# A hybrid encoder layer: a new order of the feed-forward's first tiles on PE, DVE, ACT and POOL

## The reference, cut to what matters

```python
def _dwconv3(h, conv_w, conv_b):
    hp = jnp.pad(h, ((0, 0), (1, 1), (0, 0)))
    return hp[:, :-2] * conv_w[0] + h * conv_w[1] + hp[:, 2:] * conv_w[2] + conv_b

    x = x + jnp.concatenate([attn, pool], axis=-1) @ w_out
    up = _dwconv3(_rmsnorm(x, norm2) @ w_up, conv_w, conv_b)
    gate, val = up[..., :D_FF], up[..., D_FF:]
    x = x + (jax.nn.silu(gate) * val) @ w_down
```

## Time and profile before

| | |
|---|---|
| median of 3 runs | 1142.33 us |
| profiled execution: time, span | 1145.8 us, 1144.0 us |
| PE busy | 1117.0 us (98%) |
| DVE busy | 833.3 us (73%) |
| ACT, POOL busy | 555.3 us (49%), 466.8 us (41%) |
| mean granted clock of PE | 0.994 of full |
| feed-forward's first tiles | about 371 to 442 us of the span |

### The profile page before, as it was taken

The page is one execution under the profiler, slowest core; times in us unless marked ns, Lnnn a source line. Parts: engine busy times, 40 slices in busy tenths (PEclk is TensorE's granted clock), DMA queues, the critical chain, the costliest instruction groups (busy, mean ns, idle before and its releaser), DMA issues.

```text
span 1144.0 us, 15838 instructions
## 1 busy us (share of the span) xinstructions
PE 1117.0 (98%) x5146; PEld 898.0 (78%) x5146; DVE 833.3 (73%) x1171; ACT 555.3 (49%) x986; POOL 466.8 (41%) x405
## 2 busy tenths in 40 slices
PE   8999999999999989999999999999999999999996
PEld 7788766665878867888888888888888888888885
DVE  6895976674468799878787878787876756757555
ACT  5412687775223454545454445444554545544332
POOL 0186642322567046765686568655220202211000
PEclk9999999999999999999999999999999999999999
DMA  6601000104653126443544354444896565534341
GB/s 208 222 26 44 1 12 12 38 19 168 200 185 120 56 64 220 165 139 136 194 165 138 138 193 165 138 141 173 326 349 205 186 200 189 180 100 127 92 143 74
DMA packets 138431, 161.60 MB, mean 141 GB/s; under 512 B 8755, under 2 KB 105354, under 8 KB 133770
## 3 DMA queue, kind: packets, MB, share of 16 engines
q1 hardware_dynamic: 138080, 160.82, 42.1%
q10 hardware_dynamic: 298, 0.11, 0.0%
HBM read 115.55 MB, written 45.35 MB: 141 GB/s over the span
## 4 chain that ended last, share of the span: by engine, by line
PE 84%; DVE 11%; issue 2%; ACT 1%; POOL 1%; DMA 1%; ACTq 0%; DVEq 0%; POOLq 0%
PE ps L312 26%; PE ps L313 25%; PE ps L314 25%; PE ps L885 2%; PE ps L866 2%; DVE WL L2076 1%; DVE SF L2175 1%; DVE SF L2183 1%; PE ps L877 1%; DVE XL L1745 1%; DVE WDHL L1933 1%; DMA TL<-g_scratch 1%; DVE col L1944 1%; DVE XT L1739 0%; DVE R L1926 0%
## 5 line engine op out<-in xcount | busy, mean ns | idle before, releaser
L312 PE MATMUL ps<-XH,WH 128*128 128x512 f32 x722 | 284.0, 393 | 1.4 <-DVE WL L353 1.0
L314 PE MATMUL ps<-XH,WL 128*128 128x512 f32 x722 | 281.4, 390 | 0.0
L313 PE MATMUL ps<-XL,WH 128*128 128x512 f32 x722 | 281.3, 390 | 0.0
L312 PEld LDWEIGHTS ps<-XH,WH 128*128 128x128 f32 x722 | 135.9, 188 | 31.1 <-DVE WL L353 1.8
L314 PEld LDWEIGHTS ps<-XH,WL 128*128 128x128 f32 x722 | 135.6, 188 | 28.5
L313 PEld LDWEIGHTS ps<-XL,WH 128*128 128x128 f32 x722 | 135.9, 188 | 27.2
L312 PE MATMUL ps<-GHL,WH 128*128 128x512 f32 x394 | 153.7, 390 | 1.0 <-DVE WL L2076 0.7
L314 PE MATMUL ps<-GHL,WL 128*128 128x512 f32 x394 | 153.3, 389 | 0.0
L313 PE MATMUL ps<-GHL,WH 128*128 128x512 f32 x394 | 153.3, 389 | 0.0
L348 ACT ACTIVATE WH<-WR 128x1024 fp32r<-128x1024 f32 (+3 forms) x45 | 45.5, 1012 | 135.8 <-PE ps L314 122.7
L1492 ACT ACTIVATE SF<-ps,col 128x512 f32<-128x512 f32 x88 | 68.2, 778 | 74.7 <-PE ps L314 65.6
(11 more groups left out here) (259 smaller groups left out, 2263.7 us busy)
## 6 DMA issues: line engine op xcount, KB each, us to landing
TL<-in_w_up SPq DMA_DIRECT2D x48, 256.0 KB, 3.5
s_scratch<-XT SPq DMA_DIRECT2D x11, 1024.0 KB, 4.7
XT<-in_w_down SPq DMA_DIRECT2D x11, 1024.0 KB, 6.5
t_scratch<-XT SPq DMA_DIRECT2D x11, 1024.0 KB, 3.8
WR<-t_scratch SPq DMA_DIRECT2D x44, 256.0 KB, 2.8
TL<-s_scratch SPq DMA_DIRECT2D x44, 256.0 KB, 2.9
WR<-in_w_up SPq DMA_DIRECT2D x40, 256.0 KB, 3.4
WR<-in_w_down SPq DMA_DIRECT2D x33, 256.0 KB, 3.5
```

The costliest lines, as they stand in the source:

```text
L312: pe.matmul(out, wh, xh, start=first, stop=False, skip_group_check=skip)
L313: pe.matmul(out, wh, xl, start=False, stop=False, skip_group_check=skip)
L314: return pe.matmul(out, wl, xh, start=False, stop=last, skip_group_check=skip)
```

## The change

Six edits, all around the first tiles:

- PE: the four pairs of sums by ones stood one behind the other; now an inner step of `whole(0)` (three matmuls) stands between each two pairs, three steps in all.
- ACT: one element goes through Silu ahead of the second sequence's high halves, so that the table is loaded there. Three high halves of "7" come before `copy_m5`, behind a wait for the end of `whole(3)`. The high halves of two weights come between those of "4". The weights of "6" and "5" come ahead of the activations, and `silu(0, 1, 1)` goes into the next block.
- DVE: the low half 14 comes ahead of the first taps; 15 and 16 come between the low halves of "4"; 17 and 18 between and behind the taps of tiles 2 and 3; the last two pairs of taps of f = 1 go into the next block, around its low half 20, and `add_c22` goes ahead of 21 and 22 there.
- POOL: the wait for all low halves of "4" (`b_lo` 32) ahead of the weight sums of step 1 goes.

```diff
@@ PE, sums by ones
                 ins = pe.matmul(ps[6][:, TT + t:TT + t + 1], SQT[:, t * P:(t + 1) * P], ones[:, 0:1], start=False, stop=True)
+                if t < TT - 1:
+                    whole(0, [2 + t])
             ins.then_inc(ss_ready, 1)
-            whole(0, range(2, KT))
+            whole(0, range(5, KT))
@@ ACT
             up_hi(quarter(1, 1), raw_in[1][1], 32, wo_ready, 2 * KT, 3)
+            act.activation(col[:, FR:FR + 1], ones[:, 0:1], ACT.Silu)
...
             whole_centre(0)
+            act.wait_ge(m_done, WHOLE_DONE[3])
+            for k in range(3):
+                piece_hi(MOVE["7"][0][:, k, :], xt[:, XS[1], k, :], tp_ready, k + 1)
             copy_m5(0, 1, False)
             up_hi(s1_buf(0), ws_ready, 8, m_done, entry_at("5"), 1)
-            for k in range(4):
-                piece_hi(MOVE["7"][0][:, k, :], xt[:, XS[1], k, :], tp_ready, k + 1)
+            piece_hi(MOVE["7"][0][:, 3, :], xt[:, XS[1], 3, :], tp_ready, 4)
...
                 piece_hi(MOVE["4"][0][:, k, :], xt[:, XS[0], 4 + k, :], t4_ready, k + 1)
-            up_hi(quarter(0, 1), raw_in[0][1], 64, m_done, entry_at("2"), 3)
-            up_hi(quarter(0, 0), raw_in[0][0], 64, m_done, entry_at("7"), 0)
-            for c in range(2, 4):
-                whole_centre(c)
+                if k == 0:
+                    up_hi(quarter(0, 1), raw_in[0][1], 64, m_done, entry_at("2"), 3)
+                if k == 1:
+                    up_hi(quarter(0, 0), raw_in[0][0], 64, m_done, entry_at("7"), 0)
+            whole_centre(2)
             up_hi(S2, ws_ready, 10, m_done, entry_at("3"), 1)
+            whole_centre(3)
+            up_hi(s1_buf(0), ws_ready, 9, m_done, entry_at("4"), 2)
             silu(0, 0, 0)
             silu(0, 0, 1)
             gate0(0, 1, False)
-            up_hi(s1_buf(0), ws_ready, 9, m_done, entry_at("4"), 2)
...
             copy_m1(1, 0)
-            silu(0, 1, 1)
...
                 gate0(i, f, copied=copied)
+                if copied:
+                    silu(0, 1, 1)
@@ DVE
             piece_lo("7", 3, xt[:, XS[1], 3, :])
+            up_lo(quarter(1, 3), 2, 14)
...
                 piece_lo("4", k, xt[:, XS[0], 4 + k, :])
-            up_lo(quarter(1, 3), 2, 14)
-            for k in range(2, 4):
-                piece_lo("4", k, xt[:, XS[0], 4 + k, :])
             up_lo(quarter(0, 1), 3, 15)
+            piece_lo("4", 2, xt[:, XS[0], 6, :])
             up_lo(quarter(0, 0), 0, 16)
-            for c in range(2, 4):
-                tap_left(0, 0, c)
-                tap_right(0, 0, c)
+            piece_lo("4", 3, xt[:, XS[0], 7, :])
+            tap_left(0, 0, 2)
+            tap_right(0, 0, 2)
             up_lo(S2, 1, 17)
+            tap_left(0, 0, 3)
+            tap_right(0, 0, 3)
+            up_lo(s1_buf(0), 2, 18)
             product(0, 0, 1)
             product(0, 0, 0)
-            tap_left(0, 1, 0)
-            tap_right(0, 1, 0)
-            up_lo(s1_buf(0), 2, 18)
-            for c in range(1, 4):
+            for c in range(2):
                 tap_left(0, 1, c)
                 tap_right(0, 1, c)
...
                 if behind:
+                    tap_left(0, 1, 2)
+                    tap_right(0, 1, 2)
                     up_lo(quarter(f, 1), UP_SLOT["3"], i * 14 + (base + 6))
+                    tap_left(0, 1, 3)
+                    tap_right(0, 1, 3)
+                    add_c22(i, f)
...
-                add_c22(i, f)
+                if not behind:
+                    add_c22(i, f)
@@ POOL
             pool.wait_ge(uw_lo, 13)
-            pool.wait_ge(b_lo, 32)
```

## The result

The changed kernel takes 1149.68 us (median of 6 runs, 1146.79 to 1151.15) where the kernel before takes 1142.28 (6 runs beside it): the ratio is 1.005, 95% interval 1.0036 to 1.0065, that is 5.7 us slower (4.1 to 7.4). The two medians alone lie 7.4 us apart, at the upper end of that interval; in the larger sets beside the experiments the kernel before has medians of 1143.7 to 1144.0. The profiled execution has a span of 1147.4 us against 1144.0.

A forecast was written before the change was run, and what follows sets the result against it. PE, busy 98% of the span, bounds the kernel, with DVE setting the pace in the feed-forward's first tiles. Terms 0.0 + 3.2 + 0.8 = +4.0 us on the median 1142.33 gave 1146.3, range 1138.0 to 1149.0.

The forecast's parts named there:

- Part 1: Sums by ones on PE: spacing holds the clock, but the gain goes into waiting for the diagonal; 0.0 us.
- Part 2: High halves in ACT's gaps: DVE 0.6 us earlier, POOL's four sums start at 408.6 instead of 409.22.
- Part 3 at "4": DVE's low halves take turns with POOL's sums, 1.68 us each; product "4" comes 2.0 us later.
- Part 3 at "1" of the second block: DVE's low half for product "1" lands at 444.6 against 441.17, and PE waits; term +3.2 us.
- 1.0 us in which DVE waits for ACT: Added to DVE's time before the second block: ACT work queued behind the weight that waits for "4".
- The clock: Behind "4", PE falls to 1.2 GHz after two waits of 2.5 us; +0.8 us, bounds 0 and +2.
- DVE keeps the port: Rival at "4": DVE's six instructions end near 416 and the order works as drawn; -5.8, 1136.5; chance 0.16.
- Fewer collisions: Rival: "4" ends near 421 but DVE makes it up before the second block; +1.5, 1143.8; chance 0.18.
- The clock falls at the spread too: Rival to the spaced sums: clock falls at the spread, 1.7 us later for all behind; +5.7, 1148.0; chance 0.06.

The follow-up runs named there:

- kernel 1: Changed kernel with POOL's wait for all low halves of "4" put back ahead of its weight sums; ratio to the kernel before 1.0036.
- kernel 3: Changed kernel with POOL's four weight sums taken over 4 columns instead of 512, the rest left uncomputed; ratio to the kernel before 1.0003.
- kernel 4: Changed kernel with the last two pairs of taps and the sum of blocks put back ahead of the block; ratio to the kernel before 1.0022.
- 6: Changed kernel with both POOL's wait and the last two pairs of taps put back; ratio to the kernel before 1.0007.
- kernel 2: Kernel before with only POOL's wait for the low halves of "4" removed; ratio to the kernel before 1.0008.
- 10: Kernel before with only the last two pairs of taps, their block sum and activation moved into the block; ratio to the kernel before 1.0018.
- 11: Kernel before with only the sums by ones spaced by three groups of three matmuls; ratio to the kernel before 1.0008.
- 12: 9 with the change's three groups of matmuls in the sums by ones instead of one; ratio to the kernel before 0.998.
- 7: Kernel before with only one group of three matmuls in the middle of the sums by ones; ratio to the kernel before 1.0006.
- 9: Second reordering of DVE and ACT, POOL waiting for three halves of "4", one matmul group in the sums; 1139.48 us against 1143.96 before, ratio 0.9962.
- 8: First reordering of DVE and ACT, POOL waiting for three halves of "4", one matmul group in the sums; ratio to the kernel before 0.9993.

## Why the prediction was right in its direction and low in its size

Forecast: 4.0 us slower, 1146.3, range 1138.0 to 1149.0. Measured: 5.7 slower by the ratio, which on the forecast's base of 1142.33 is 1148.0, inside the range; the median of 1149.68 itself lies 0.7 us above it.

- **Part 1, 0.0: right, the reason half right.** F went from 7.62 to 7.32, with no slow matmul and a wait of 1.18 us where 1.3 was forecast; the 0.3 us are that the sums ended 2.06 us later and not 2.34. What I had wrong is the clock's fall as a fixed property of sums in a row: it came in two of four profiles.
- **Part 2, DVE 0.6 us earlier: right.** POOL's four sums start at 405.95 + 2.35 = 408.30 (forecast 408.6), the first half of "4" at 412.23 (412.5). Of the 0.92 us by which the four sums are earlier, 0.30 is the shorter F, which leaves 0.6.
- **Part 3 at "4": right nearly to the tenth.** On the clock of before, POOL's first weight sum starts at 414.16 (forecast 414.3), DVE's instructions stand 1.68 apart (1.68), the last half ends at 421.46 (421.6), and PE takes it at 421.51 (421.65). The Trainium skill's "SBUF — State Buffer", section "Who interferes with whom", has the loser wait for the whole instruction; by that I had estimated a turn of 1.97 us. The row's 1.68 decides: that one engine blocks the other is as the Trainium skill says, the price of a turn is not. Kernels 1 and 3 show that POOL's sums are the cause.
- **Part 3 at "1" of the second block: mechanism right, too small.** The weight landed at 443.75 + 2.35 = 446.10, forecast 444.6. The term that failed is "1.0 us in which DVE waits for ACT": DVE stood still for 0.93 + 1.96 + 0.64 = 3.53, the first two for ACT and the last for PE. The clock and the taps make this together: without the slow matmuls behind "4" it is 0.93 (kernel 3), with the taps back in their place 0.41 (kernel 4). The slow matmuls made product "5" late, which the sum needs; and I had counted the taps as moved work, not as work that before filled DVE's waits. The collisions behind came out 1.0 us under mine (0.94, 1.09, 0.7 and 0.2 for three of 1.08 and 0.7), which is no more than the kernel before had there (2.93 us in both). That the wait of 2.19 us came out inside the forecast's 2 to 3 is partly luck: PE, too, was late there, at 441.70 + 2.35 = 444.05 where 441.4 was forecast, about what thirteen slow matmuls cost (2.6 us). From the spread to this product PE lost 66.45 - 61.66 = 4.8 us, against 3.2 + 0.8: roughly 4.0 us are waits for DVE (7.64 against 3.63), about 1.0 is thirteen slow matmuls behind "4" instead of eight.
- **The clock, +0.8 with a bound of +2: right behind "4", missed at the second place.** It fell twice. The spell behind "4" (419.2 to 424.4, clock 0.50) I had foreseen, and it costs 1.0 us more than that of before; the one behind the wait of 2.19 us at "1" of the second block I had not, though I forecast that very wait at 2 to 3 us and had a row with a fall behind 2.15 us. Its eight slow matmuls cost 1.6 us, but the kernel before waits 0.55 us there for a block's sum, and the changed one does not: a hundred matmuls further on the changed kernel has lost 0.8 of the 5.75 - 4.8 + 0.3 = 1.25 us that are left. The other 0.4 lies later and is not explained. Kernel 4, where that wait is gone, has no slow matmuls there, and neither has 6.
- **Rivals.** "DVE keeps the port" fell: none of the five instructions ran at 0.68. "Fewer collisions" fell: DVE made nothing up, its weight landed 4.9 us later than before. "The clock falls at the spread too" did not come: behind that wait the clock held in seven profiles of seven.

How far the causes add up: alone in the kernel before, the wait costs 0.9 us, the taps 2.1 and the spaced ones 0.9 (the first and last not told from nothing), 3.9 in all, against 5.7. With intervals of 1 us and more to either side on each of these, the two are not clearly apart. That the causes make each other worse is argued from the traces and not shown by the times: in the new order two weights stand among the halves of "4" under POOL's sums, and there POOL's wait is worth 4.3 us of PE's waits in "4" (5.4 against 1.1, kernel 1), in the old order 1.1 (kernel 2). I have not split the rest further.

## What to carry to other kernels

Before an engine's sums are released earlier, list what the other engine runs beside them: two engines that take turns can both be free of waits and still make the third wait. An instruction that fills a neighbour's wait is not free to move; look at what its engine would do there instead, and at who is queued behind its new place. Every wait that a forecast puts on PE needs a clock term of its own.

## What the runs showed of the hardware that I had not expected

- **Turns cost the two sides unequally.** Alone, DVE's instructions start 0.60 us apart (two take 1.28 us at 415.77, one 0.68) and POOL's sums 1.37 (416.41 and 417.78 in kernel 1); in turns both start 1.68 apart in the changed kernel. POOL loses 0.31 us per turn, DVE 1.08.
- **The clock is not settled by the instructions alone.** The same one-column sums in a row were followed by the lower level in two profiles of four; waits of 2.06 to 2.17 us in "4" in four of six (before, 10, 11 and 12; not 7 and 9); waits of 1.14 to 1.19 us at the spread in none of seven; yet in 8 two waits of 1.20 and 0.84 us with three matmuls between them were followed by it. A difference of some 1.5 us between two single profiles of these kernels can be this alone. The Trainium skill, in "TensorE: Matmul & The Clock Gate", Part 1, calls the number of slow matmuls at a kernel's start run-variable for one and the same kernel. Here the slow matmuls lie in the middle of a kernel, and what varies between two profiles of the same stretch of code is whether they come at all.
